# A hybrid decoder step on one core: weight sums of the first gate-up block on another engine, later queue order, and one output tile finished a chunk sooner

## The reference

```python
xp = xp + g1 * mix_out(...)                  # attention and convolution, output projection
h  = modulate(xp, ln2_g, sh2, sc2)           # (576 tokens, 1024)
g, u = jnp.split(h @ w_gu, 2, axis=-1)       # w_gu (1024, 2*2816)
y  = xp + g2 * ((jax.nn.silu(g) * u) @ w_down)   # w_down (2816, 1024)
```

## Time and profile before

| | |
|---|---|
| median of 3 runs | 944.64 us (943.31 to 945.0) |
| profiled execution, device time | 946.95 us |
| its span | 945.1 us |
| TensorE busy | 914.5 us (97%) |
| VectorE, ScalarE, GpSimd busy | 635.1, 406.2, 289.8 us (67%, 43%, 31%) |
| granted TensorE clock, mean | 0.992 |

### The profile page before, as it was taken

One profiled execution on the slowest core, in us unless ns is written; L12 is line 12 of the kernel. 1 busy time (PEld: TensorE's weight loads), 2 busy tenths in 40 slices (PEclk: granted clock), 3 DMA queues, 4 the chain that ended last, 5 costly groups with the idle time before them and its releaser, 6 DMA issues.

```text
span 945.1 us, 16421 instructions
## 1 busy us (share of the span) xinstructions
PE 914.5 (97%) x6253; PEld 763.5 (81%) x6253; DVE 635.1 (67%) x1242; ACT 406.2 (43%) x818; POOL 289.8 (31%) x281
## 2 busy tenths in 40 slices
PE   6999999999999999999999997999999999999997
PEld 5778878999996666776744497999999999888886
DVE  3556674598738777667422898999888898444434
ACT  3664562231146334767600673444444446323220
POOL 4112000000024442535400336777777774000000
PEclk9999999999999999999999998999999999999999
DMA  8997512254339896393103162433333333522201
GB/s 271 390 373 264 177 50 89 89 160 191 124 101 373 332 337 221 91 300 90 35 1 111 73 173 61 119 90 90 90 92 103 108 101 112 190 90 89 72 1 51
DMA packets 84187, 138.83 MB, mean 147 GB/s; under 512 B 4179, under 2 KB 54947, under 8 KB 79758
## 3 DMA queue, kind: packets, MB, share of 16 engines
q1 hardware_dynamic: 74578, 96.26, 31.7%
q0 software_dynamic: 9248, 41.39, 12.5%
q10 hardware_dynamic: 284, 0.13, 0.1%
HBM read 130.58 MB, written 11.31 MB: 150 GB/s over the span
## 4 chain that ended last, share of the span: by engine, by line
PE 81%; DVE 8%; DMA 4%; issue 3%; ACT 3%; POOL 1%; SPq 0%; DVEq 0%; ACTq 0%; POOLq 0%
PE bank L2331 16%; PE bank L2333 16%; PE bank L2332 16%; PE bank L2325 8%; PE bank L2411 3%; PE bank L2845 3%; PE bank L2855 3%; PE bank L2692 2%; DMA wring<-in_w_ada 2%; PE bank L2662 2%; PE bank L2360 2%; PE bank L2825 2%; PE bank L2341 2%; PE bank L2340 2%; PE bank L2616 2%
## 5 line engine op out<-in xcount | busy, mean ns | idle before, releaser
L2331 PE MATMUL bank<-s,ring_hi 128*128 128x288 f32 x620 | 185.0, 298 | 5.9 <-issue 4.3
L2332 PE MATMUL bank<-s,ring_lo 128*128 128x288 f32 x620 | 183.9, 297 | 0.0
L2333 PE MATMUL bank<-s,ring_hi 128*128 128x288 f32 x620 | 183.2, 296 | 0.0
L2331 PEld LDWEIGHTS bank<-s,ring_hi 128*128 128x128 f32 x620 | 117.1, 189 | 6.7 <-issue 4.5
L2333 PEld LDWEIGHTS bank<-s,ring_hi 128*128 128x128 f32 x620 | 117.8, 190 | 0.0
L2332 PEld LDWEIGHTS bank<-s,ring_lo 128*128 128x128 f32 x620 | 117.3, 189 | 0.0
L521 DVE TENSOR_TENSOR ring_lo<-mem,ring_hi 128x512 fp32r<-128x512 f32 x84 | 107.7, 1299 | 0.0
L2325 PEld LDWEIGHTS bank<-cst,arena 128*128 128x128 f32 (+1 forms) x538 | 61.5, 146 | 21.3 <-issue 12.6
L2325 PE MATMUL bank<-cst,arena 128*128 128x128 f32 (+1 forms) x538 | 71.1, 285 | 7.8 <-DMA arena<-in_cache_k_cmp,idx 6.6
L893 POOL DMA_INDIRECT arena<-in_cache_k_slc,idh x16 | 15.4, 964 | 172.8 <-PE bank L2333 167.3
L521 DVE TENSOR_TENSOR dn_w<-wring,dn_w 128x2048 fp32r<-128x2048 f32 (+1 forms) x11 | 23.1, 2097 | 65.9 <-ACT dn_w L518 65.9
(11 more groups left out here) (363 smaller groups left out, 2092.8 us busy)
## 6 DMA issues: line engine op xcount, KB each, us to landing
wring<-in_w_gu SPq DMA_DIRECT2D x44, 512.0 KB, 5.2
wring<-in_w_ada SPq DMA_DIRECT2D x16, 1024.0 KB, 12.3
wring<-in_w_in SPq DMA_DIRECT2D x10, 1024.0 KB, 5.1
wring<-in_w_down SPq DMA_DIRECT2D x10, 1024.0 KB, 5.1
wring<-in_w_ada SPq DMA_DIRECT2D x16, 512.0 KB, 8.5
proj<-in_x_prompt SPq DMA_DIRECT2D x4, 512.0 KB, 12.7
mem<-in_state_k_win POOLq DMA_DIRECT2D x8, 256.0 KB, 8.6
mem<-in_state_v_win POOLq DMA_DIRECT2D x8, 256.0 KB, 6.6
```

Source lines behind the costliest of these rows:

```text
L2331: pe.matmul(dst, sh, ml, start=first and k == 0, stop=False)
L2332: pe.matmul(dst, sl, mh, start=False, stop=False)
L2333: ins = pe.matmul(dst, sh, mh, start=False, stop=last and k == len(pairs) - 1)
```

## The change

Three edits, all in the order of queues and the place of work. First, the four weight sums of block 1 ((1,7), (1,5), (1,6), (1,4)) are made by VectorE (`first_made`) and no longer by GpSimd; GpSimd now waits, after its token sums, until `sums_low(2, 3)`, the last split of a token sum, is done, and then goes on with its loop. Second, the VectorE and ScalarE queues at the entry are reordered: the splits of slots 6, 8 and 9 and the last three token splits `sums_low(s, 3)` change places. Third, in down, chunk i = 4 of each n is taken in the order (0, 1, 2, 4, 3), and right after tile 4 the same tile's product of the last chunk is computed, so that the last chunk has only the tiles (0, 1, 2, 3).

```diff
@@ GpSimd
             sums(0)
-            for m in (7, 5, 6):
-                make(1, m)
+            pool.wait_ge(seg_low, SEG_LOW.index((2, 3)) + 1)
             for p, (f, m) in enumerate(FAST):
...
-                if 0 < p < NFAST - 8 and FAST[p + 8][1] >= 4:
+                if 2 < p < NFAST - 8 and FAST[p + 8][1] >= 4:
                     make(*FAST[p + 8])
@@ ScalarE
             plain_silu(2, c21)
+            slot_cast(8)
+            slot_cast(9)
             for s in range(3):
                 sums_high(s, 3)
-            slot_cast(8)
-            slot_cast(9)
             first_copy(2)
@@ VectorE
+            def first_made(m):
+
+                weights(dve, ("gu", 1, 0))
+                want_slot(dve, AT[1, m])
+                dst = slot(AT[1, m])[0]
+                if m == 7:
+                    ins = dve.tensor_tensor(dst, block_of(1, 3), block_of(1, 0), ALU.subtract)
+                elif m == 5:
+                    ins = dve.tensor_tensor(dst, block_of(1, 0), block_of(1, 1), ALU.subtract)
+                elif m == 6:
+                    dve.wait_ge(made, MADE[1, 5])
+                    ins = dve.tensor_tensor(dst, block_of(1, 3), slot(AT[1, 5])[0], ALU.subtract)
+                else:
+                    dve.wait_ge(made, MADE[1, 6])
+                    ins = dve.tensor_tensor(dst, slot(AT[1, 6])[0], block_of(1, 2), ALU.subtract)
+                ins.then_inc(made, 1)
+
             plain_product(1, c11s[0], actT[:, 0, 0:HALF])
-            slot_rest(6)
             sum_made(2, 5)
+            first_made(7)
             sums_low(1, 5)
             sum_made(2, 7)
+            slot_rest(6)
             slot_rest(7)
...
             sum_made(1, 3)
             sum_made(2, 3)
+            slot_rest(8)
+            slot_rest(9)
...
             sums_low(2, 7)
-            for s in range(3):
-                sums_low(s, 6)
+            sums_low(0, 6)
+            first_made(5)
+            sums_low(1, 6)
+            first_made(6)
+            sums_low(2, 6)
+            first_made(4)
             first_result(1)
-            slot_rest(8)
-            slot_rest(9)
             plain_product(3, c21, actT[:, 0, HALF:TOK])
             slot_rest(10)
-            for s in range(3):
-                sums_low(s, 3)
             slot_rest(11)
             first_result(2)
             slot_rest(12)
+            for s in range(3):
+                sums_low(s, 3)
             slot_rest(13)
@@ TensorE, down
-                for t in DN_ORDER:
+                for t in (DN_ORDER, (0, 1, 2, 4, 3), (0, 1, 2, 3))[max(0, i - 3)]:
                     if i == 0:
                         want_free(pe, ("dn", n, t))
                     ins = down(n, t, j, range(nk), i == 0, i == 5)
                     if i == 5:
                         fills(ins, ("dn", n, t))
+                    if i == 4 and t == 4:
+                        pe.wait_ge(lo_ready, j + 1 - NFT)
+                        fills(down(n, t, j + 1, range(down_job(j + 1)[3]), False, True), ("dn", n, t))
                 if i < 5:
                     ins.then_inc(dn_read, 1)
```

## The result

The changed kernel took 940.01 us (median of 16 runs, 938.38 to 942.44) against 947.27 (943.31 to 950.18, 16 runs) of the kernel before on the same chip: a ratio of 0.9928, interval 0.9914 to 0.9942. The profiled execution has a span of 937.7 us, against 945.1.

The account below looks back on a forecast made before the run. TensorE, busy 914.5 of 945.1 us, was taken as the bound, leaving its pauses, clock and ends. Gate-up 5.4 - 2.0 = 3.4, plus 1.2 at the end, gives 4.6 us: 940.0 against 944.64, range 937.0 to 942.2.

Parts of the forecast that it names:

- Part 1: Pause before `gp` 2: with GpSimd idle VectorE's three token splits end sooner, so `gp` 2 starts 1.0 us earlier.
- Part 2: VectorE up to (1,6): splits ready in time, the pause there goes, 5.5 us gained, and 2.2 us of slow clock.
- Part 3: Block 2, after GpSimd's later release: (2,7) 0.5 us late, new 3.0 us pause at (2,4), which still starts 5.4 us earlier.
- The price of a turn: GpSimd and VectorE alternate on SBUF, one instruction each; GpSimd's instruction takes about 1.23 us, then VectorE's own.
- Part 4: Clock behind the new pause at (2,4): slow stretch costs 2.0 us, bounds 0 and 3.2.
- Part 5: Down: VectorE meets the last tiles as they come, so the end is 1.2 us sooner; bounds 0 and 1.3.
- A: The forecast itself: pause at (2,4) of 2 to 3.5 us, clock down once behind it; 940.0 us, chance 0.55.
- B: Same pause at (2,4), but the clock stays up; gain 6.6 us, 938.0 us, chance 0.15.
- C: Pause at (2,4) stays under 1 us, VectorE getting more turns or GpSimd's short instructions coming sooner; 935.0 us, chance 0.10.
- D: VectorE late for (1,5) by up to 2.8 us, the clock falls a second time; gain 2.4 us, 942.2 us, chance 0.14.
- E: Ring of waits: late product (3,1) delays GpSimd's sums and (2,4); slower from 4.6 us late, 946.0 at 6; chance 0.06.

Follow-up runs that it names:

- the first sum alone: Kernel before with one edit: GpSimd's sum (1,7) waits until sums_low(2, 4) is done; 944.91 us, ratio 1.0007.
- the fill kernel: Changed kernel with GpSimd's four sums of weight block 3 replaced by zero fills, result incomplete; 936.6 us, ratio 0.991 to the kernel before.
- the sums alone moved and (3,5) later: Kernel before with block 1's sums on VectorE, GpSimd's wait, down edit, old queue order, and sum (3,5) waiting for split (2,7); 940.18 us, ratio 0.994.
- the sums alone: Kernel before with block 1's four sums on VectorE, GpSimd's new wait and the down edit, in the old queue order; 939.21 us, ratio 0.9926.
- the entry alone: Changed kernel with the down edit undone; 939.36 us, ratio 0.9944 to the kernel before.
- the changed kernel again: Changed kernel, unaltered, run once more on the chip of the other runs of its set; 941.63 us, ratio 0.995 to the kernel before.
- the order alone: Changed kernel with block 1's four sums back on GpSimd and without its new wait, keeping queue orders and down edit; 940.84 us, ratio 0.9961.

## Why the prediction was right, step by step

The time, 940.0 forecast and 940.01 measured, was right to a degree that is luck: the median on which it rests, 944.64 of three runs, was 947.27 over sixteen. The gain was too small in the profiled pair: 4.6 us forecast, 5.6 measured. Over the other profiles it is 4.9 to 6.8, by the first ratio 6.8 (5.5 to 8.1), by the second, on another chip, 4.7 (2.8 to 6.6). In the pair, (2,4) starts 5.8 us sooner behind matmul 3601 where 5.4 was forecast, what follows takes back 1.5 instead of 2.0, and the end gives 1.24 instead of 1.2.

- Part 1, 1.0 us: 0.96 (74.32 us from matmul 3601 to `gp` 2 before, 73.36 after). Shown by the first sum alone too.
- Part 2: right nearly to 0.1 us. Counted from `gp` 2, the split of (1,5) was forecast to be done at 12.0 and is done at 12.0 (562.94 - 550.93); GpSimd's release was forecast at 15.1 and is at 15.07. No pause before (1,5) to (1,4).
- Part 3, right in kind and in the place of the long pause, too dear in size: 0.5 at (2,7) and 3.0 at (2,4) were forecast, 0.22 at (2,6) and 2.36 at (2,4) measured. The link that came out otherwise is `t_sum`. I took 1.1 us behind a turn of VectorE, so that it ended 7.9 us behind GpSimd's release and held VectorE's sum for m = 3. It took 0.81 at once, since VectorE was itself waiting for sum (2,4), and ended at 7.1. The split of (2,6) then had its turn behind it and was done at 7.7 instead of 7.2: that is the short pause, one product sooner than said, and it is this split, not `t_sum`, that held the sum for m = 3, to 7.6. From there the five instructions took 5.9 us for 6.0 forecast. In all (2,4) starts 28.6 us behind `gp` 2 instead of 29.1.
- The price of a turn, "about 1.23 us", is too large for its own rows: from the end of VectorE's instruction at 583.59 to that of GpSimd's at 584.74 they give 1.15. In the changed kernel a turn adds 1.07 to 1.10 us to VectorE's instruction. The sum of part 3 was made from whole durations, so it doesn't rest on it. That the pause is made of turns is shown by the fill kernel.
- Part 4, the clock, 2.0 us: 1.19 in the profile in which it fell, 0 in the one in which it didn't. It is the term most mis-sized. That the loop behind the pause is the one before holds to 0.3 us: from (2,4) to matmul 4201 the kernel before takes 21.30 us, the changed one without a fall 21.57.
- What I had not weighed is that the kernel before has a fall of its own whose length varies: I priced it at 2.2 us from one profile, and in a second one it was 0.7 us less.
- Part 5, 1.2 us: 1.24, and nothing lost at either wait.
- Rivals: A is what the profile shows, and B what the second profile of the same kernel shows; that the two are one kernel in different executions I had not seen, I had taken them for alternatives. C (a pause under 1 us) came only in other kernels: without GpSimd's reads there is no pause at (2,4), and with the sums alone moved and (3,5) later it is 0.23, with 0.77 and 0.92 at other places. D and E, VectorE late for (1,5) or (3,1), didn't come: both splits were in time.
- What I had not asked is whether the second edit is needed. The prediction took the queue order as part of what removes the pause before (1,6); the sums alone do that, and with the new order the stretch is 0.5 us longer.

## What to carry to other kernels

Where VectorE and GpSimd both read SBUF, an instruction moved from GpSimd to VectorE can shorten VectorE's own queue: here 0.6 us is added and a turn of 1.1 taken away. Carry the durations of the rows forward through the queues until the next instruction is late: the long pause that replaces the one removed was found in this way, in its place and to 0.6 us. And before a gain of a few us is put down to a change, look how often and how long the clock fell in each profile: the same entry with the same pauses gave 129.08 and 128.38. Last, test the halves of an edit that has two: one of them can be doing all the work.

## What the runs showed of the hardware

- A pause of 2.35 us of TensorE was followed by 1.2 GHz in two profiles (the changed kernel, the entry alone) and by 2.4 GHz in two (the changed kernel again, the order alone). Pauses of 4.25 to 4.49 us were followed by 1.2 GHz in all three profiles that have one; pauses up to 1.62 us in gate-up in none.
- How long TensorE then works at 1.2 GHz varies too: behind pauses of 4.26 and 4.25 us it was 5.0 us in one profile and 3.4 in the other, a difference of 0.7 us in time.
- Most of the scatter of a kernel's runs goes with its mean granted clock. The changed kernel's 16 runs, by mean granted clock: 0.998: 938.4 us (3 runs), 0.996: 939.9 (6), 0.995: 941.5 (6), 0.993: 942.4 (1). The kernel before ran 61 times beside the experiments; its four largest groups are 0.995: 943.5 (18), 0.993: 945.1 (18), 0.992: 946.7 (8), 0.991: 945.5 (5). A straight line in the mean clock takes up three quarters of the variance of the 61. A part of a low mean costs nothing: in the profile before the clock is at 0.50 for the last 2.2 us of the span, behind the last matmul.
- A GpSimd fill of 128x512 took 0.53 us and left VectorE's two-input instructions at 0.44 to 0.68 us, while subtractions of the same size by GpSimd made each of them 1.07 to 1.10 us longer.
